# S5 branch of a three-branch layer: shared first steps of the phase tables, products of two tiles issued together, states turned back in place

## What is computed

```python
def s5_branch(u, a_re, a_im, log_dt, b_re, b_im, c_re, c_im, d_skip, w_glu):
    ug = u.reshape(bsz, seq, N_SSM_GROUPS, SSM_GROUP)          # 64 groups of 16 channels
    ...                                                        # ab = exp(dt * (lam_r + i lam_i)), bb = f * b
    x_r = jnp.einsum('bsgc,gpc->bsgp', ug, bb_r)               # 64 states for each group
    x_i = jnp.einsum('bsgc,gpc->bsgp', ug, bb_i)
    _, _, h_r, h_i = lax.associative_scan(_complex_affine_combine, (a_seq_r, a_seq_i, x_r, x_i), axis=1)
    y = (jnp.einsum('bsgp,gcp->bsgc', h_r, c_re) - jnp.einsum('bsgp,gcp->bsgc', h_i, c_im))
    y = y + d_skip.reshape(N_SSM_GROUPS, SSM_GROUP) * ug
    z = jax.nn.gelu(y.reshape(bsz, seq, D_SSM)) @ w_glu
```

## Time and profile before

| | us |
|---|---|
| median of 3 runs | 3366.08 (3359.88 to 3367.69) |
| profiled execution, its own time | 3367.36 |
| its span | 3365.6 |
| S5 beside the stream, first product to last | about 1605 to 2340 |
| PE busy, share of the span | 95% |
| mean granted TensorE clock | 0.972 |

### The profile page before, as it was taken

How to read it: one execution, slowest core, us unless ns; L and a number is a source line. 1 busy time by engine, 2 the same in 40 slices (tenths; PEclk the granted TensorE clock), 3 DMA queues, 4 the chain that set the end, 5 groups by cost and what they waited for, 6 DMA issues and landing times.

```text
span 3365.6 us, 54085 instructions
## 1 busy us (share of the span) xinstructions
PE 3195.7 (95%) x21726; PEld 2917.0 (87%) x21726; DVE 2287.2 (68%) x3156; ACT 1841.0 (55%) x2371; POOL 674.8 (20%) x1110
## 2 busy tenths in 40 slices
PE   6989898999999999998999998989999999999998
PEld 6889888889999999887887887888998888888887
DVE  6655788656778777656656676666566788888554
ACT  5544778545666666553555544333545666666443
POOL 1000000000000000114656777774001000000000
PEclk9999999999999999999999999889999999999999
DMA  5445444555455555555333433434555555555554
GB/s 195 145 132 178 137 149 153 195 191 197 169 170 174 170 171 191 179 180 192 132 113 117 134 126 127 137 126 146 205 183 187 188 191 191 188 192 190 188 191 140
DMA packets 158045, 560.53 MB, mean 167 GB/s; under 512 B 17552, under 2 KB 25808, under 8 KB 157152
## 3 DMA queue, kind: packets, MB, share of 16 engines
q1 hardware_dynamic: 157792, 557.06, 49.3%
HBM read 550.64 MB, written 6.36 MB: 165 GB/s over the span
## 4 chain that ended last, share of the span: by engine, by line
PE 70%; DVE 11%; POOL 8%; ACT 7%; issue 3%; DMA 1%; SPq 0%; DVEq 0%; ACTq 0%; POOLq 0%
PE ps L561 70%; POOL TB L1917 4%; DVE WL L1329 3%; ACT WH L901 2%; ACT L891 2%; POOL PT L1917 2%; POOL BX L1917 1%; POOL BS L1917 1%; DVE HH L1292 1%; DVE X L1303 0%; DMA scratch<-X 0%; DVE BS L1319 0%; DVE XC L1303 0%; DVE XV L1303 0%; DVE XC L1319 0%
## 5 line engine op out<-in xcount | busy, mean ns | idle before, releaser
L561 PE MATMUL ps<-XN,WH 128*128 128x256 f32 (+1 forms) x8864 | 1876.7, 305 | 47.6 <-DVE WL L1329 25.7
L901 ACT ACTIVATE WH<-RAW 128x1024 fp32r<-128x1024 f32 x1010 | 1065.5, 1057 | 1266.7 <-PE ps L561 1232.8
L1329 DVE TENSOR_TENSOR WL<-RAW,WH 128x1024 fp32r<-128x1024 f32 x1010 | 1262.5, 1256 | 499.4 <-ACT WH L901 492.8
L561 PEld LDWEIGHTS ps<-XN,WH 128*128 128x128 f32 x8864 | 1447.6, 194 | 137.8 <-DVE WL L1329 28.5
L561 PE MATMUL ps<-XN,WL 128*128 128x256 f32 x5120 | 1453.8, 284 | 0.0
L561 PEld LDWEIGHTS ps<-XN,WL 128*128 128x128 f32 x5120 | 989.0, 193 | 0.0
L561 PE MATMUL ps<-YS,WH 128*128 128x512 f32 (+1 forms) x1088 | 369.9, 388 | 4.7 <-DVE YS L1292 2.2
L1917 POOL TENSOR_TENSOR RSB<-RSB,SQ 128x256 f32<-128x256 f32 x75 | 75.0, 1000 | 1212.4 <-ACT SQ L891 1211.2
L561 PE MATMUL ps<-YS,WL 128*128 128x256 f32 x1056 | 296.5, 281 | 0.0
L561 PEld LDWEIGHTS ps<-YS,WH 128*128 128x128 f32 x1088 | 202.8, 189 | 49.0 <-DVE YS L1292 2.5
L1917 POOL TENSOR_TENSOR SQ<-SQ 128x512 f32<-128x512 f32 (+1 forms) x24 | 33.1, 1378 | 1052.5 <-ACT SQ L891 1051.5
(11 more groups left out here) (328 smaller groups left out, 3438.1 us busy)
## 6 DMA issues: line engine op xcount, KB each, us to landing
RAW<-in_w SPq DMA_DIRECT2D x1010, 512.0 KB, 3.3
CSB<-sums SPq DMA_DIRECT2D x64, 128.0 KB, 3.7
scratch<-X SPq DMA_DIRECT2D x2, 2048.0 KB, 7.9
X<-scratch SPq DMA_DIRECT2D x2, 2048.0 KB, 7.8
X<-in_x SPq DMA_DIRECT2D x4, 512.0 KB, 7.6
X<-in_x SPq DMA_DIRECT2D x1, 2048.0 KB, 9.2
out<-X SPq DMA_DIRECT2D x4, 512.0 KB, 2.6
WIF<-in_w_if SPq DMA_DIRECT2D x1, 576.0 KB, 14.4
```

The costliest lines, as they stand in the source:

```text
L561: return pe.e.matmul(dst, l, r, start=start, stop=stop, skip_group_check=True)
L901: act.e.activation(WH[:, w % NH, :], RAW[:, w % NB, :], ACT.Copy).then_inc(*act.one(("wh", w)))
L1329: dve.e.tensor_tensor(WL[:, w % NB, :], RAW[:, w % NB, :], WH[:, w % NH, :].bitcast(F32), SUB).then_inc(*dve.one(("wl", w)))
```

## The change

- **Tables.** At step 0 to 3 POOL builds the first 16 positions of the phase tables of all 32 tiles at once (PB). A pair's table is then a copy of 16 columns and four levels of six instructions: 16, 32, 64 and 128 new columns for each of the two tiles. The last level is no longer cut in halves.
- **Pairs.** The chain goes by pairs of tiles: pair m starts at step 9 + 10m, ten steps to a pair. At r = 0 PE takes two side banks and issues BR of both tiles, then BI of both; at r = 10 CR of both, then CI of both. The two tiles' operands lie in different 32-row groups of the array (BR, BI), and their results in different 32-column groups (CR, CI).
- **Steps.** ACT copies at r = 1 and 2; the multiplications by cos and sin come at r = 2 and 3; sum and scans at r = 4 and 5; POOL's multiplications by sin at r = 5 and 6; the turning back at r = 7 and 8; PE at r = 10; the skip term at r = 12 after every second pair.
- **Buffers.** BS gets a second buffer, HH goes: states are turned back in BS. ACT's copy for tile n now waits for the products (`sy`) of tile n - 2, since PE reads them from BS.
- **End.** The chain has 178 steps: gelu at 173, the copy at 175, the rest at 177.

```diff
-    "dv": 1, ... "gl": 2, "s5": 197, "wo": 1,
+    "dv": 1, ... "gl": 2, "s5": 178, "wo": 1,
...
             def s5(s):
-                for n, r in s5_tiles(s):
+                for m, r in s5_pairs(s):
+                    ft = m // 2
+                    pair = [(n, slice(32 * (n % 4), 32 * (n % 4) + 32)) for n in (2 * m, 2 * m + 1)]
                     if r == 0:
-                        b = take("side", "bu", n)
+                        b = [take("side", "bu", n) for n, _ in pair]
...
-                        mm(b[:, 0:256], BR[rows, ft, :], US[rows, ft, :])
-                        mm(b[:, 256:512], BI[rows, ft, :], US[rows, ft, :]).then_inc(*pe.one(("bu", n)))
-                    if r == 6:
+                        for c, src in ((slice(0, 256), BR), (slice(256, 512), BI)):
+                            for i, (n, rows) in enumerate(pair):
+                                x = mm(b[i][:, c], src[rows, ft, :], US[rows, ft, :])
+                        x.then_inc(*pe.one(("bu", 2 * m), ("bu", 2 * m + 1)))
+                    if r == 10:
...
-                        pe.wait_ge(*at("hh", n))
+                        pe.wait_ge(*at("hh", 2 * m + 1))
...
+                        for c, src in enumerate((CR, CI)):
+                            for n, rows in pair:
+                                x = mm(b[rows, 0:256], src[:, n, :], BS[n % 2][:, c, :], c == 0, c == 1)
...
-            def phases(b, r):
+            def rotate(tb, n, l, tiles, *names):
+                d = 1 << l
+                c, s_ = [PW[:, i, l, tiles].unsqueeze(2).to_broadcast([128, n, d]) for i in range(2)]
+                t = PT[:, 0:n * d].rearrange("p (n a) -> p n a", n=n)
+                x, y = slice(0, d), slice(d, 2 * d)
+                tt(tb[:, 0, :, y], tb[:, 0, :, x], c, MUL)
+                tt(t, tb[:, 1, :, x], s_, MUL)
+                tt(tb[:, 0, :, y], tb[:, 0, :, y], t, SUB)
+                tt(tb[:, 1, :, y], tb[:, 0, :, x], s_, MUL)
+                tt(t, tb[:, 1, :, x], c, MUL)
+                tt(tb[:, 1, :, y], tb[:, 1, :, y], t, ADD, *names)
...
+                if s < 4:
+                    rotate(PB, 32, s, slice(0, 32))
+                m, r = divmod(s - 4, 10)
+                if s >= 4 and m < 16 and r in (0, 1, 2, 4):
...
+                        pool.e.tensor_copy(tb[:, :, :, 0:16], PB[:, :, 2 * m:2 * m + 2, :]).then_inc(*pool.one())
+                    rotate(tb, 2, {0: 4, 1: 5, 2: 6, 4: 7}[r], slice(2 * m, 2 * m + 2), ("tb", m))
...
-def s5_tiles(s):
-            r = s - (11 + 11 * (n // 2) + 5 * (n % 2))
+def s5_pairs(s):
+    return [(m, s - 9 - 10 * m) for m in range(16) if 0 <= s - 9 - 10 * m < 13]
```

More of the change, by code:

```diff
@@ L457, in build @@
         BX = [v3(m(f"BX{i}", 512), 2) for i in range(2)]
-        BS = v3(m("BS", 512), 2)
-        HH = v3(m("HH", 512), 2)
-        PT = m("PT", 2 * 64)
+        BS = [v3(m(f"BS{i}", 512), 2) for i in range(2)]
+        PT = m("PT", 256)
         CUM = m("CUM", 256)
@@ L1205, in s5 @@
             def s5(s):
-                for n, r in s5_tiles(s):
-                    if r == 1:
-                        b = bank("bu", n)
+                for m, r in s5_pairs(s):
+                    if r in (1, 2):
+                        n = 2 * m + r - 1
+                        b, i = bank("bu", n), n % 2
                         act.wait_ge(*at("bu", n))
                         if n > 1:
[L1211 to L1218, removed]
+                            act.wait_ge(*at("sy", n - 2))
+                        fn(BX[i], v3(b, 2), ACT.Copy)
+                        fn(BS[i][:, 0, :], b[:, 256:512], ACT.Copy)
+                        fn(BS[i][:, 1, :], b[:, 0:256], ACT.Copy, ("bx", n), ("free", "bu", n), scale=-1.0)
+                if s == 173:
                     act.wait_ge(*at("usd", 7))
                     fn(US, US, ACT.Gelu_apprx_tanh, ("gelu",))
-                if s == 194:
-                    act.wait_ge(*at("bss", 31))
+                if s == 175:
                     fn(ZS[:, :, 0:256], US, ACT.Copy, ("zsh",))
@@ L1791, in s5 @@
             def s5(s):
[L1792 to L1798, removed]
+                for m, r in s5_pairs(s):
+                    n = 2 * m + {2: 0, 3: 1, 4: 0, 5: 1, 7: 0, 8: 1}.get(r, 0)
+                    x, y = BX[n % 2], BS[n % 2]
+                    c2 = TB[:, m % 2, 0, n % 2, :].unsqueeze(1).to_broadcast([128, 2, 256])
+                    if r in (2, 3):
@@ L1815, in s5 @@
-                    if r == 7 and q_ == 3:
-                        dve.wait_ge(*at("sy", n))
+                            scan(y[:, c, :], mg, x[:, c, :], 0.0, MUL, ADD, ("scn", n))
+                    if r in (7, 8):
+                        dve.wait_ge(*at("bss", n))
+                        tt(y, y, c2, MUL, ("hhc", n))
+                        tt(y[:, 0, :], y[:, 0, :], x[:, 0, :], SUB)
+                        tt(y[:, 1, :], y[:, 1, :], x[:, 1, :], ADD, ("hh", n))
+                    if r == 12 and m % 2:
+                        ft = m // 2
+                        dve.wait_ge(*at("sy", 2 * m + 1))
@@ new lines, in s5 @@
+            def s5(s):
+                if s == 0:
+                    pool.wait_ge(*at("pw"))
+                    fill(PB[:, 0, :, 0:1], 1.0)
+                    fill(PB[:, 1, :, 0:1], 0.0)
+                if s < 4:
+                    rotate(PB, 32, s, slice(0, 32))
+                m, r = divmod(s - 4, 10)
+                if s >= 4 and m < 16 and r in (0, 1, 2, 4):
+                    tb = TB[:, m % 2]
+                    if r == 0:
+                        if m > 1:
+                            pool.wait_ge(*at("hhc", 2 * m - 3))
+                        pool.wait_ge(*pool.last)
+                        pool.e.tensor_copy(tb[:, :, :, 0:16], PB[:, :, 2 * m:2 * m + 2, :]).then_inc(*pool.one())
+                    rotate(tb, 2, {0: 4, 1: 5, 2: 6, 4: 7}[r], slice(2 * m, 2 * m + 2), ("tb", m))
+                for m, r in s5_pairs(s):
+                    n = 2 * m + {2: 0, 3: 1, 5: 0, 6: 1}.get(r, 0)
+                    x, y = BX[n % 2], BS[n % 2]
+                    ss = TB[:, m % 2, 1, n % 2, :]
+                    if r in (2, 3):
@@ L1987, in s5 @@
-                b, r = divmod(s, 11)
-                if b < 16 and r < 9:
-                    phases(b, r)
+                        tt(x[:, 0, :], y[:, 1, :], ss, MUL)
+                        tt(x[:, 1, :], y[:, 0, :], ss, MUL, ("bss", n))
             walk(lambda t, k, a, b: None, lambda u: None, {
```

63 lines of the change are left out of this document (10 added, 53 removed), and 2 rows, old and new, of the table STEPS.

## The result

The changed kernel takes 3276.64 us (median of 4 runs, 3274.07 to 3279.52); the kernel before took 3366.89 us beside it. The ratio is 0.9735, interval 0.9723 to 0.9747. The forecast was 3282. The profiled execution has a span of 3277.7 us at a mean granted clock of 0.980, against 3365.6 us at 0.972: 87.9 us less. It was the slowest of the four, whose spans are 3272.3 to 3277.7 us at mean clocks of 0.983 to 0.980.

What follows compares the result with a forecast made beforehand. It took PE's stream of weight blocks as the bound, with POOL setting the pace in S5's pairs. 40.6 + 33 + 22 + 3 - 14 = 84.6 us off 3367.4 gave 3282 us, range 3246 to 3332.

Steps and rivals of the forecast that it cites:

- HH waits: PE's waits for HH in S5, 40.6 us in all, would go but for small ones.
- Half clock: PE's half-clock time behind the waits in S5's two stretches would go, worth 33 us.
- 0.98 and more: Sign: the granted clock in S5's stretches rises to this from 0.94 and 0.90.
- The end: Gelu, copy and rest move 18 units earlier, beside the stream, so PE's wait for ZS goes: 3 us.
- What is added: New side-bank, HH and WL waits, mainly in the attention part: 14 us lost, bounds 0 and 45.
- rival 3: PE stands waiting for side banks in the attention part; at 20 such places 3410 us; chance 0.06.
- The sum: All terms of the forecast together: 84.6 us gained.
- the products: A pair's eight products break PE's stream once: 22 us gained, 11 without overlap, 39 by the skill's figure.
- 1 (no overlap): PE's products of two tiles do not overlap: 11 instead of 22 us, 3293; counted within the forecast's 0.70.
- 2 (DVE): DVE takes over as the bound, its steps 2 us late in each pair: 3325 us; chance 0.20.
- 4: HH waits go, but PE waits for the weight stream instead, no gain: about 3366 us; chance 0.04.
- 480: Sign: POOL's busy time in all falls from 675 to about 480 us.

Runs made afterwards that it cites:

- tables_alone: Kernel before with only the shared table PB and the new pair tables; steps, buffers and products as before: 3341.6 us, ratio 0.9923.
- tables_step_later: tables_alone with PE's CR and CI products, and the skip term behind them, one step later: 3290.3 us, ratio 0.977.
- late_end: Changed kernel with gelu, copy and rest put back right ahead of `gg`, at steps 192, 194 and 196: 3283.6 us, ratio 0.9756.
- us_tile_by_tile: Changed kernel, but PE issues BR and BI of the first tile, then BR and BI of the second: 3278.5 us, ratio 0.9744.
- cc_same_columns: Changed kernel, but the second tile's CR and CI products write into the first tile's 32 output rows: 3284.6 us, ratio 0.9755.

## Why the prediction was right, point by point

- **HH waits, 40.6 taken.** 7.8 stayed for BS: 32.8 gone. That they would go I had from POOL's occupation and the chain together; tables_alone and tables_step_later show that the step of margin weighs at least as much. In the kernel before, two causes lay over each other: faster tables alone give 25 us, with the step 77.
- **Half clock, 33.** The clock's loss in PE's busy time fell from 74.6 to 50.2: 24.4, 9 less than taken. The changed kernel's four executions differ by 5.4 us in span, so a part of this is chance. The first stretch stayed at 0.95, where I had said 0.98 and more.
- **The end, 3.** Idle time 3.2 less as said; late_end pays 7 us for it in the changed kernel.
- **What is added, -14 (0 to -45).** PE's idle time fell by 27.0, where 40.6 + 3.2 had gone: 16.8 us of waits stayed or came, 7.8 for BS and 9 net of others (GE 5.6, ACT's BS 3.6 and the like). The side ring (rival 3) shows as a single wait of 3.6 us.
- **The sum** was 84.6, measured 87.9: the products gave 17.2 more; the clock's 8.6, the 2.8 of added waits and the unexplained 2.7 took most of it back. The time was right to 0.2%, by errors that cancel: the waits went as said, but the closeness is luck.
- **Rivals.** 1 (no overlap) is refuted by the timeline. 2 (DVE): in the pair's 30.9 us DVE is busy 28.3, yet PE doesn't wait; of 16 pairs five wait, 7.8 us in all, among them three of the last four. 3 and 4 didn't occur.
- **POOL.** Its busy time is 539.8, not 480. The 480 doesn't follow from the prediction's own terms: 16 x 23.4 for the pairs, 15.8 for PB and the 120.5 us that POOL is busy outside S5's time (88.2 ahead of 1540 us, 32.3 behind 2345) make 511. The rest is the tables. The shared one took POOL from 1545.3 to 1568.0 us and cost PE nothing, since the first use was at 1609.8.

The row of 64 columns taken for 32 and 64 was too low, and that of 256 too high. Three of the tables' groups after (busy us, mean ns, idle before):

```profile
L1915 POOL TENSOR_TENSOR PT<-TB,PW 128x32 f32<-128x32 f32 x32 | 15.2, 474 | 2.5
L1915 POOL TENSOR_TENSOR PT<-TB,PW 128x64 f32<-128x64 f32 x32 | 22.9, 715 | 2.5
...
L1915 POOL TENSOR_TENSOR PT<-TB,PW 128x256 f32<-128x256 f32 x32 | 29.9, 933 | 2.5
```

Over all groups the means are 514, 686, 677 and 972 ns for 32, 64, 128 and 256 columns, where I had 396 twice, 699 and 1139: 17.1 us for a pair's table instead of 15.8.

## What to carry to other kernels

Small products that use a part of the array's rows or columns should stand together when they lie in different groups: two cost what one does, and the order within the four or eight made no difference here. More than two groups at once weren't tried. When a wait is to go, ask two questions of its producer, how much it has to do and how many steps lie between its last instruction and the consumer. Here a faster producer alone gave 25 us, one step more on top of it another 51, and in the SSD stage one buffer more gave nothing. Test each half of a change alone and then both, since two causes of one wait show little until both are gone.

## What the runs showed of the hardware

- f32 products overlap, at no cost above 0.02 us for the second tile, in groups of 32 rows (1.06 against 1.92 us for four), of 32 columns with all 128 rows (0.99 against 1.85), and of 64 columns (eight in the 0.80 us of four).
- Two groups don't wait for each other's order: in us_tile_by_tile the second tile's BR starts 0.014 us behind the first tile's, ahead of the first tile's BI, which was issued before it.
- A wait of 3.2 us was followed by 6 us at clock 0.50 in one kernel (late_end) and by none in another, the kernel before, whose clock was 1.00 there; behind one wait of 3.62 us at 1858 us the changed kernel ran at half clock and cc_same_columns at full.
- 88 us more work on POOL cost PE 27 us, most of it in the pairs behind the attention part, where POOL had little time to spare.
